# ScalarE copies a finished projection before it rounds the next weight piece

## The chip, the cores and the metric

The kernel runs on one core of one Trainium2 chip. The metric is device time in microseconds (us), the median of the runs. Three runs of the kernel before took 1799.23, 1800.72 and 1801.95 us; the median is 1800.72 us.

## What is computed

Two transformer stacks run one after the other on a sequence of 256 tokens of width 1024, batch 1, in fp32. The first has two layers, each with a mixer (compressed, selected and windowed attention, stick-breaking attention and forgetting attention), cross attention to a memory of 256 tokens, and a gated MLP of width 2816 with a causal convolution over three tokens. The second has a retention layer with a context of 256 tokens, then a layer whose mixer is a gated short convolution; both are followed by a SwiGLU MLP of width 2816. The parts that matter here:

```python
# first stack, MLP
u = causal_conv3(h @ w_up, conv_w) + conv_b
gate, val = u[..., :D_FF], u[..., D_FF:]
return (jax.nn.silu(gate) * val) @ w_down
# second stack, mixer of the second layer
b_gate, c_gate, xv = jnp.split(h @ w_in, 3, axis=-1)
return (b_gate * short_conv(c_gate * xv, w_conv)) @ w_out
# second stack, both MLPs
return (jax.nn.silu(h @ w1) * (h @ w3)) @ w2
```

## The kernel before, in words

Activations lie in SBUF with features on partitions and the 256 tokens on the free axis. All weights come as a stream of 532 pieces of 128x1024 fp32 (512 KB), which SyncE loads into a ring of eight slots (`ring`). TensorE multiplies in fp32r, so each piece and each activation is cut into a rounded upper part and a remainder. ScalarE rounds a piece into `WH[s]` (`split`, L447) and VectorE subtracts to get `WL[s]` (`split`, L813). There are two buffers of each, s = 0 and 1. The product takes upper times upper, upper times lower and lower times upper.

The work is a fixed table of 28 stages (`STAGES`). A stage that makes projections (`make` on TensorE) turns a piece into 128 output features: 8 x 2 matmuls with `WH[s]`, then 8 with `WL[s]`, into PSUM bank `proj[s]`, and then it raises `mm_done`. A step of the loop is two pieces, s = 0 and s = 1. Before a piece TensorE waits for `wh_ready` and for `bank_free[s]`; before the last eight matmuls it waits for `consumed`, which VectorE raises with `WL[s]`. A stage that adds (`add`: out, mo, down, ro, f2, co) accumulates in four other banks and has no projection to copy out. Where a stage starts on freshly normed activations, its first step runs both pieces interleaved (`fresh=True`).

Each engine runs its own written order. `weights` on ScalarE (the function that the change touches) does for each piece: wait for `mm_done`, run `before` where there is one, round the next piece of that s (`split`), run `evac` where there is one. The `evac` that the stages give:

- q, kv, mq, rq: copy `proj[s]` out (L483) and free the bank. rg: the same with Silu (L746). rk: 512 columns (L751).
- rv (`values`, L757): wait for TensorE's four transposes of the piece before, then copy 512 columns.
- up (`up_upper`, L479): at s = 0, round the previous step's product into FH. The taps `up` (L701, L704) are its `before`.
- f13 (`swiglu`): at s = 0, Silu of `proj[0]` (L725); at s = 1, wait for VectorE's product (`bank_free[1]`), then round it into FH (L728).
- cx (`conv_in`, L786): at s = 0, wait for the product of the step before, then copy `proj[0]` out.
- cb (`conv_upper`, L797): wait for VectorE's product of this piece (`bank_free[s]`), then round it into FH. Its `before` is `conv_gate` (L792).

The stage mkv has its own loop, which the change does not touch.

VectorE's `weights` does for each piece: `before` (in cb: two taps L1230 and the product L1233; in f13 at s = 1 the product L1134), `split` (which waits for `wh_ready`), `evac` (in cb and f13 the remainder FL, L1237 or L895), and in some stages a reduction over an extra piece for the modulation vectors (`ada`, L821, L823). In the last step of a stage both engines round the first two pieces of the next stage.

Of the kernel before, what the change touches and what calls it, by code (L numbers as in the profile page):

```python
# [55 lines left out]
def next_piece(st, i, s):  # L56

    return i * st["per"] + (st["base"] + s * (st["per"] // 2))
# [138 lines left out]
def transformer(nc, xT_d, memT_d, ctxT_d, cond_d, stream_d, vecs_d, const_d, rope1_d, rope2_d, decay_d,  # L197
# [5 lines left out]
    with ctx:  # L203
# [180 lines left out]
        def loop(eng, steps, step, chain=None, per=0, peel=False):  # L384


            if peel:
                step(0, False)
            if steps > 1:
                with eng.Fori(1 if peel else 0, steps - 1) as i:  # L390
                    if chain:
                        chain.enter(i, per)
                    step(i, False)
                if chain:
                    chain.leave(steps - 1)
            step(steps - 1, True)
# [43 lines left out]
        def _(act):  # L440
# [4 lines left out]
            def split(r, s):  # L445
                act.wait_ge(loaded, r + 1)
                A(WH[:, s, :], ring[:, r % RING, :], ACT.Copy).then_inc(wh_ready, 1)  # L447

            def weights(k, evac=None, per=0, peel=False, before=None, tail=None, after=None):


                st = TABLE[k]

                def step(i, last):
                    for s in range(2):
                        if last and s == 1 and tail:
                            tail()
                        act.wait_ge(mm_done, i * 2 + (st["p0"] + s + 1))
                        if before:
                            before(i, s)  # L460
                        if not last:
                            split(next_piece(st, i, s), s)
                        elif k + 1 < len(TABLE):
                            split(TABLE[k + 1]["r0"] + s, s)
                        if evac:
                            evac(i, s)
                if after:
                    for i in range(st["steps"]):
                        step(i, i + 1 == st["steps"])
                        after(i)  # L470
                else:
                    loop(act, st["steps"], step, chain, per, peel)
                if evac:
                    n["q"] += st["steps"]
# [1405 lines left out]
```

## Time and profile before

| | us |
|---|---|
| median of three runs | 1800.72 |
| the profiled execution's own time | 1801.96 |
| its span | 1800.0 |
| TensorE matmul busy | 1701.6 (95%) |
| VectorE busy | 1107.1 (62%) |
| ScalarE busy | 827.6 (46%) |
| rounding on ScalarE, L447, 436 pieces | 461.0, mean 1057 ns |
| remainder on VectorE, L813, 436 pieces | 533.0, mean 1223 ns |

Span and own time differ by 1.96 us, which lies around the first and the last instruction. The mean granted TensorE clock is 0.976 of full speed. Busy time of an engine is a sum over all stages; which engine binds has to be read stage by stage. In the rows below a start is in us from the span's start, a duration is in us, and the last bracket is the idle time of the engine ahead of the row and who ended it. A row with x1 is one instruction. Instructions of one engine overlap a little: the next starts about 0.1 us before the recorded end of the one ahead.

### The profile page before, as it was taken

To read this page: it belongs to the slowest core of one execution; us is meant where nothing else is said; L and a number is where in the kernel's file an instruction comes from. 1 tells how busy PE (TensorE), PEld (TensorE's weight loads), DVE (VectorE), ACT (ScalarE), POOL (GpSimd) and SP (SyncE) were. 2 spreads that over 40 slices of the span, in tenths; PEclk is the share of its full clock that TensorE was granted. 3 is DMA by queue.
4 is the path that set the end of the run, shared out by engine and by line. 5 is a ranking of instruction groups with operands and counts; after the bars stand their busy time and mean duration, and the time that the engine had idled before them with its cause. 6 is when DMAs were issued, how large, how long until landed. Compare 5 with 4: busy or idle time off the path is not lost.

```text
span 1800.0 us, 37316 instructions
## 1 busy us (share of the span) xinstructions
PE 1701.6 (95%) x12659; PEld 1554.6 (86%) x12678; DVE 1107.1 (62%) x1644; ACT 827.6 (46%) x1392; POOL 38.8 (2%) x43
## 2 busy tenths in 40 slices
PE   8989989999898998999979999799899999999998
PEld 6976869999797676999959888589799988989998
DVE  3536468888773645888866632447755564665544
ACT  4545556653453555665344322113544444454443
POOL 0020000000002000000000000200000000000000
PEclk9988999999998999999999999999999999999999
DMA  9520225558783021556927842116555674445551
GB/s 321 176 72 1 85 68 167 183 187 274 219 268 106 1 94 47 176 186 200 372 107 237 300 152 93 58 47 231 201 182 180 222 256 140 163 134 182 186 182 64
DMA packets 81229, 293.41 MB, mean 163 GB/s; under 512 B 9360, under 2 KB 10768, under 8 KB 80400
## 3 DMA queue, kind: packets, MB, share of 16 engines
q1 hardware_dynamic: 78768, 283.29, 46.4%
q10 hardware_dynamic: 2400, 9.27, 1.8%
q8 instruction: 42, 0.69, 0.2%
q14 instruction: 19, 0.16, 0.0%
HBM read 291.48 MB, written 1.05 MB: 163 GB/s over the span
## 4 chain that ended last, share of the span: by engine, by line
PE 77%; DVE 10%; ACT 6%; issue 4%; DVEq 1%; POOL 1%; ACTq 0%; SPq 0%; DMA 0%; POOLq 0%
PE projs L1316 51%; PE accs L1316 20%; PE ob L1316 4%; ACT WH L447 3%; DVE WL L813 1%; DVE rstd L899 1%; DVE ring L823 1%; PE projs L1505 1%; DVE scr L905 1%; DVE cprod L821 1%; ACT scr L489 1%; DVE AL L914 1%; ACT AH L507 0%; DVE x L837 0%; DMA ring<-in_stream 0%
## 5 line engine op out<-in xcount | busy, mean ns | idle before, releaser
L813 DVE TENSOR_TENSOR WL<-ring,WH 128x1024 fp32r<-128x1024 f32 x436 | 533.0, 1223 | 472.4 <-ACT WH L447 471.8
L447 ACT ACTIVATE WH<-ring 128x1024 fp32r (+1 forms) x436 | 461.0, 1057 | 606.7 <-PE projs L1316 376.6
L1316 PE MATMUL projs<-AH,WH 128*128 128x256 f32 (+1 forms) x2432 | 626.4, 295 | 30.3 <-ACT AH L507 9.6
L1316 PE MATMUL projs<-AL,WH 128*128 128x256 f32 (+1 forms) x2432 | 629.8, 296 | 1.3
L1316 PEld LDWEIGHTS projs<-AH,WH 128*128 128x128 f32 x2432 | 463.2, 193 | 46.6 <-issue 26.3
L1316 PEld LDWEIGHTS projs<-AL,WH 128*128 128x128 f32 x2432 | 462.8, 193 | 22.4 <-DVE AL L912 7.1
L1316 PE MATMUL projs<-AH,WL 128*128 128x256 f32 (+1 forms) x2432 | 361.9, 292 | 1.4 <-DVE WL L813 1.4
L1316 PEld LDWEIGHTS projs<-AH,WL 128*128 128x128 f32 x2432 | 325.9, 193 | 9.0 <-DVE WL L813 1.6
L1316 PE MATMUL accs<-FH,WH 128*128 (+1 forms) x768 | 187.8, 282 | 0.2
L1316 PE MATMUL accs<-FL,WH 128*128 (+1 forms) x768 | 187.9, 281 | 0.0
L1316 PEld LDWEIGHTS accs<-FH,WH 128*128 128x128 f32 x768 | 144.4, 188 | 1.1 <-issue 1.1
L1316 PEld LDWEIGHTS accs<-FL,WH 128*128 128x128 f32 x768 | 145.1, 189 | 0.0
L823 DVE SCALAR_TENSOR_TENSOR ring<-ring,crow 128x1024 f32 (+1 forms) x96 | 117.1, 1220 | 2.6
L1316 PE MATMUL accs<-FH,WL 128*128 (+1 forms) x768 | 112.2, 281 | 0.0
L1316 PEld LDWEIGHTS accs<-FH,WL 128*128 128x128 f32 x768 | 100.1, 189 | 0.0
L701 ACT ACTIVATE cv<-projs,vecs 128x256 f32<-128x256 f32 x88 | 49.6, 564 | 91.8 <-PE projs L1316 91.8
L1316 PE MATMUL ob<-scr,const 128*128 128x256 f32 x224 | 61.7, 428 | 18.4 <-ACT scr L489 17.6
L1316 PE MATMUL accs<-AH,WH 128*128 (+1 forms) x288 | 72.9, 286 | 2.5 <-DVE AL L970 1.9
L1316 PEld LDWEIGHTS ob<-scr,const 128*128 128x128 f32 x224 | 45.9, 214 | 31.2 <-ACT scr L489 24.2
L1316 PE MATMUL accs<-AL,WH 128*128 (+1 forms) x288 | 72.1, 283 | 0.0
L1316 PEld LDWEIGHTS accs<-AH,WH 128*128 128x128 f32 x288 | 55.2, 192 | 4.6 <-DVE AL L970 3.1
L1316 PEld LDWEIGHTS accs<-AL,WH 128*128 128x128 f32 x288 | 55.2, 192 | 0.0
(217 smaller groups left out, 1555.9 us busy)
## 6 DMA issues: line engine op xcount, KB each, us to landing
ring<-in_stream SPq DMA_DIRECT2D x532, 512.0 KB, 4.2
W1v<-in_w ACTq DMA_DIRECT2D x4, 512.0 KB, 8.1
W1k<-in_w ACTq DMA_DIRECT2D x4, 512.0 KB, 12.7
D<-in_decay ACTq DMA_DIRECT2D x4, 512.0 KB, 3.3
x<-in_xT SPq DMA_DIRECT2D x2, 512.0 KB, 5.2
memT<-in_memT SPq DMA_DIRECT2D x1, 1024.0 KB, 11.2
ctxT<-in_ctxT ACTq DMA_DIRECT2D x1, 1024.0 KB, 5.9
out_y<-ybuf SPq DMA_DIRECT2D x8, 128.0 KB, 2.0
```

The costliest lines, as they stand in the source:

```text
L447: A(WH[:, s, :], ring[:, r % RING, :], ACT.Copy).then_inc(wh_ready, 1)
L489: A(scr1[:, kb % 4, :], src[:, kb, :], ACT.Square).then_inc(sq_ready, 1)
L701: A(cv[:, s, :], proj[s][:, 0:S], ACT.Identity, bias=cb, scale=w2).then_inc(tap_ready, 1)
L813: V.tensor_tensor(WL[:, s, :], ring[:, r % RING, :], WH[:, s, :].bitcast(F32), ALU.subtract).then_inc(consumed, 1)
L821: chain.link(V.scalar_tensor_tensor(out=cprod[:], in0=piece, scalar=1.0, in1=crow_ctx[:], op0=ALU.mult, op1=ALU.mult, accum_out=modc[:, ba ...
L823: V.scalar_tensor_tensor(out=piece, in0=piece, scalar=1.0, in1=crow[:], op0=ALU.mult, op1=ALU.mult, accum_out=mod[:, bass.ds(j, 1)]).then_ ...
L899: chain.link(V.reciprocal((dst or rstd)[:], rms[:]))
L905: V.scalar_tensor_tensor(out=scr2[:, kb % 4, :], in0=src[:, kb, :], scalar=gain[:, kb:kb + 1], in1=by[:], op0=ALU.mult, op1=ALU.mult).then ...
L914: V.scalar_tensor_tensor(out=AL[:, kb, sel, :], in0=scr2[:, kb % 4, :], scalar=shift[:, kb:kb + 1], in1=hi, op0=ALU.add, op1=ALU.subtract) ...
L1316: return T.matmul(out, lhsT, rhs, start=start, stop=stop, skip_group_check=True)
L1505: ins = T.transpose(projs[:, g, dst:dst + 128], prob[:, g, src:src + 128], ident)
```

## The change

In `weights` on ScalarE the call of `evac` is moved ahead of the rounding of the next piece. The waits inside `evac` move with it, so that the rounding now stands behind them. Nothing else is changed; the order on TensorE, VectorE, GpSimd and SyncE is as it was.

```diff
                         act.wait_ge(mm_done, i * 2 + (st["p0"] + s + 1))
                         if before:
                             before(i, s)
+                        if evac:
+                            evac(i, s)
                         if not last:
                             split(next_piece(st, i, s), s)
                         elif k + 1 < len(TABLE):
                             split(TABLE[k + 1]["r0"] + s, s)
-                        if evac:
-                            evac(i, s)
```

## Rows read from the trace of the kernel before

**Rows 1.** The page: shares of the chain of waits by engine.

```profile
PE 77%; DVE 10%; ACT 6%; issue 4%; DVEq 1%; POOL 1%; ACTq 0%; SPq 0%; DMA 0%; POOLq 0%
```

**Rows 2.** Windows: busy us (instructions) per engine, granted clock, DMA share, GB/s.

```profile
1289.00:1411.00 122.00, 121.33 (x1011) 121.17 (x1010) 68.44 (x85) 57.31 (x86) 0.00 (x0) 1.00 0.56 180
...
1540.00:1563.00 23.00, 20.59 (x164) 19.66 (x163) 18.07 (x32) 12.21 (x20) 0.00 (x0) 1.00 0.41 140
```

**Rows 3.** Timeline of ScalarE in stage cb: start, duration, instruction, idle before.

```profile
1556.94 0.42 ACT L797 ACTIVATE FH<-prod 128x256 f32 x1 [1.84 <-DVE prod L1233]
1557.26 0.49 ACT L792 ACTIVATE cv<-CU,vecs 128x256 f32 x1
1557.66 1.04 ACT L447 ACTIVATE WH<-ring 128x1024 fp32r x1
```

**Rows 4.** Timeline of VectorE in stage cb.

```profile
1556.38 0.42 DVE L1233 TENSOR_TENSOR prod<-cv,projs 128x256 f32<-128x256 f32 x1
1556.72 1.22 DVE L813 TENSOR_TENSOR WL<-ring,WH 128x1024 fp32r<-128x1024 f32 x1
...
1558.70 0.48 DVE L1230 SCALAR_TENSOR_TENSOR cv<-CU,vecs,cv 128x256 f32<-128x256 f32 x1 [0.43 <-DVE FL L1237]
...
1559.89 0.42 DVE L1233 TENSOR_TENSOR prod<-cv,projs 128x256 f32<-128x256 f32 x1
...
1566.08 0.42 DVE L1233 TENSOR_TENSOR prod<-cv,projs 128x256 f32<-128x256 f32 x1
```

**Rows 5.** Timeline of TensorE at the start of stage co.

```profile
1565.30 1.11 PE L1316 MATMUL accs<-FH,WL 128*128 128x256 f32 x8
```

**Rows 6.** Timeline of all engines in stage f13, at s = 1.

```profile
1405.50 0.42 DVE L1134 TENSOR_TENSOR prod<-cv,projs 128x256 f32<-128x256 f32 x1 [0.36 <-PE projs L1316]
1405.54 1.06 ACT L447 ACTIVATE WH<-ring 128x1024 fp32r x1 [1.55 <-PE projs L1316]
...
1406.79 1.22 DVE L813 TENSOR_TENSOR WL<-ring,WH 128x1024 fp32r<-128x1024 f32 x1 [0.87 <-ACT WH L447]
...
1407.05 1.12 PE L1316 MATMUL projs<-AH,WL 128*128 128x256 f32 x8
```

**Rows 7.** Timeline at the first step of stage f13.

```profile
1289.41 0.36 ACT L725 ACTIVATE cv<-projs 128x256 f32<-128x256 f32 x1
1289.67 1.05 ACT L447 ACTIVATE WH<-ring 128x1024 fp32r x1
...
1289.83 0.39 PE L1316 MATMUL projs<-AH,WH 128*128 128x256 f32 x1 [0.67 <-ACT cv L725]
...
1290.87 0.41 DVE L1134 TENSOR_TENSOR prod<-cv,projs 128x256 f32<-128x256 f32 x1
```

**Rows 8.** Timeline of ScalarE and VectorE in stage up, at s = 0.

```profile
304.81 1.05 ACT L447 ACTIVATE WH<-ring 128x1024 fp32r x1
...
306.09 1.22 DVE L813 TENSOR_TENSOR WL<-ring,WH 128x1024 fp32r<-128x1024 f32 x1
...
307.94 0.48 DVE L1079 SCALAR_TENSOR_TENSOR cv<-projs,vecs,cv 128x255 f32<-128x255 f32 x1 [0.30 <-ACT cv L701]
```

**Rows 9.** Timeline of TensorE where it waits behind q, kv and rv.

```profile
499.74 1.21 PE L1316 MATMUL projs<-AH,WL 128*128 128x256 f32 x8 [1.35 <-DVE WL L813]
...
541.74 0.58 PE L1316 MATMUL projs<-AH,WH 128*128 128x256 f32 x1 [3.35 <-DVE AL L912]
...
1150.48 0.63 PE L1685 MATMUL accs<-const,scr 128*128 128x128 f32 x4 [2.22 <-DVE V L1155]
```

**Rows 10.** Timeline of ScalarE at the end of stage rv.

```profile
1148.38 0.58 ACT L757 ACTIVATE scr<-projs 128x512 f32<-128x512 f32 x1
```

**Rows 11.** Waits of TensorE over the span: total us, times, longest.

```profile
PE projs L1316 <- ACT P L483: 4.9, 2, 3.9
...
PE accs L1316 <- ACT mq L483: 0.9, 2, 0.5
```

**Rows 12.** Window at the start of stage mkv: columns as in Rows 2.

```profile
542.00:546.00 4.00, 4.00 (x20) 4.00 (x21) 0.00 (x0) 0.00 (x0) 0.42 (x1) 0.50 0.72 265
```

## Prediction

> **What bounds the kernel now.** I read the chain of waits first: 77% of it is TensorE [rows 1]. So a change on ScalarE costs or saves time only where TensorE runs out of work, and the question for each stage is how much time lies between a late piece and the matmul that needs it. The windows by stage say where that is. In f13, as in up, TensorE is busy 121.33 of 122.00 us with 1011 matmuls, 0.12 us each, so a piece of 24 matmuls takes 2.88 us and a step 5.76 us [rows 2]. In cb it is busy only 20.59 of 23.00 us [rows 2]: there it waits on something else. The timelines of single steps then give the order on ScalarE and VectorE.
>
> What a late WH[s] must meet: TensorE works on the other bank for 2.88 us after it has raised mm_done for s. Then it needs the new WH[s] and the freed bank, and 16 x 0.12 = 1.92 us later WL[s].
>
> **What the change removes, adds and moves.** No instruction is added or removed. The copy comes earlier by one rounding (about 0.96 us from start to start), the rounding later by the copy and by whatever wait stands in front of it. A 256-column ACTIVATE puts the next one 0.32 us later (1556.94 to 1557.26) [rows 3], a Silu of 256 columns 0.26 us [rows 7].
>
> *Plain copies (q, kv, rq, rg, mq; rk with 512 columns).* WH comes 0.26 us later (rk about 0.5), WL too. Against a cover of 2.88 us less one rounding that is nothing. In the first step of a stage, where TensorE waits for the copy (0.67 us idle at 1289.83) [rows 7], it needs WH as well: copy plus rounding have the same sum in either order. Cost 0. The exceptions are stage ends where TensorE is idle behind VectorE's last WL. Behind q of the second layer it waits 1.35 us for WL, and that WL ends a row of VectorE work that began with a WL after a rounding: +0.27 us. Behind both kv stages it waits for the last remainder AL, which VectorE makes after the last WL (3.35 us idle in the second layer, as much in the first): 2 x 0.28 us [rows 9]. Together +0.8 us.
>
> *mq, twice.* TensorE waits for the second copy, 0.9 us in both stages together [rows 11], and this wait goes. But VectorE's second WL comes 0.3 us later, and the first row maxima of the attention are queued behind it on VectorE. What is late next is these maxima: between -0.46 us and +0.3 us each; I take 0, since the two nearly meet.
>
> *up, 2 x 22 steps.* At s = 0 the FH rounding now stands ahead of the piece. The product is ready (the taps ahead of it have waited for it already). WH starts 0.31 us later, at 305.12, and ends 306.17; WL moves from 306.09 to about 306.35 [rows 8]. VectorE then idles 0.30 us before the next taps (307.94), and this hides the 0.26 us. TensorE needs WH only at 307.04. Cost 0. If the cover is gone, taps and product move by what is left over, still ahead of TensorE.
>
> *f13, 2 x 22 steps.* At s = 1 the piece now waits for the product, 1405.50 + 0.42. FH starts 0.14 us after it (as 1556.38 + 0.42 to 1556.94 in cb [rows 3, 4]), 1406.06; WH 1406.38 to 1407.44, instead of 1405.54 to 1406.60, 0.84 us later [rows 6]. TensorE's piece at s = 0 ends at 1407.05 + 1.12 = 1408.17, so 0.7 us are left in steady state (some 0.45 with the hop of a semaphore and the earlier issue of the weight load). WL moves from 1406.79 to 1407.63 and has 1.9 us more. Cost 0 per step. The first step is another case: the product at s = 1 stands behind WL of s = 0, which is 0.26 us late: 1291.13 to 1291.54, FH 1291.68, WH 1292.00 to 1293.05, at TensorE 1293.15. It is ready at 1289.83 + 2.88 = 1292.71 [rows 7]. +0.44 us, twice: +0.9 us.
>
> *cx.* The copy at s = 0 waits for the product of the step before, which is there as soon as the piece is. The chain of this stage runs over the rounding at s = 1, which has no evac. Its first step hands on about +0.15 us.
>
> *End of rv.* The copy waits for four transposes (0.63 us [rows 9]), then takes 0.58 us [rows 10], and the last WH and WL come behind it; TensorE waits 2.22 us for a V copy that stands behind this WL on VectorE [rows 9]. +0.9 us. Within rv a piece takes more than 5 us, and nothing is late.
>
> *cb, 8 pieces: the step that decides.* Here ScalarE now waits for VectorE's product before it rounds, and VectorE waits for the rounding before it makes WL. Two queues that ran side by side become one chain. Before: product 1556.38, WL 1556.72, FL, next taps 1558.70, next product 1559.89, 3.51 us from product to product, and WL started 0.34 us after the product since WH was long there [rows 4]. After: product ends +0.42, FH starts +0.56, WH +0.88, ends +1.92 [rows 3], and WL starts about 0.19 us after that, as in f13 (1406.60 to 1406.79 [rows 6]): +2.11. So WL, and behind it on VectorE FL, the next taps and the next product, come 1.77 us later per piece. FH, done earlier now, gives nothing back, since FL stood behind WL before, too. Seven such pieces lie ahead of the eighth product: it moves from 1566.08 [rows 4] to 1566.08 + 7 x 1.77 = 1578.5. The second piece of co is rounded 0.88 us after it starts and at TensorE 2.0 us after it: 1580.5. Before, TensorE began this piece at 1565.30 + 1.11 = 1566.41 [rows 5]. +14.1 us, and co is bound by TensorE from there, so nothing gives it back. Bounds of the unshown hops: 0.03 to 0.2 us from WH to WL, 0.26 to 0.42 us from FH to WH, that is 1.55 to 1.9 us per piece, +12.5 to +15 us.
>
> *Sum.* 0.8 + 0 + 0.9 + 0.15 + 0.9 + 14.1 = +16.8 us. Against the profiled execution's own time, 1801.96, that gives 1818.8; it lay 1.2 us above the median, so against the median 1817.5 us (+0.93%).
>
> **The clock.** After the idle 3.35 us at 541.74 the granted clock is 0.50, the 1.2 GHz level, and 20 matmuls take 4.00 us [rows 9, 12] where they take 2.4 us at full clock: 1.6 us lost in that window. In cb after the change TensorE would work 2.88 of 5.28 us and idle 2.4 us at a time, shorter than that, so I forecast full clock. Within cb a fall would mostly hide; at the start of co it would cost 1.6 to 3 us.
>
> **The rivals.**
> 1. *The clock falls in cb and stays low into co.* For it: half of each piece time becomes idle. Against it: each idle stretch is shorter than the 3.35 us of [rows 9]. 16.8 + 1.6 to 3, some 1820 us.
> 2. *cb is covered (not slower).* A piece is rounded one ahead, and a late WL in cb hides as it does in f13. Then only the edges count: 0.8 + 0.9 + 0.15 + 0.9 = +2.8 us less 0.9 us at mq, 1802.6 us. It holds as long as VectorE, not in wait for WH, has 1.77 us idle per piece. Against it: it idles 0.43 us before the taps, and this behind its own FL [rows 4].
> 3. *The bank is what counts.* TensorE's waits for copies (4.9 us for P, 0.9 us for mq [rows 11]) go with the earlier release, and cb is covered: about 1795 us. Against it: at P the same matmul needs WH, so the order there changes nothing. The Trainium skill, PSUM — Partial Sum Buffer, Summary: rules for kernel authors, says under its general entry to evacuate promptly, for want of room in the banks. By that the change is an improvement; only the mq rows of this trace bear it out.
> 4. *f13 loses in every step.* If hops were 0.5 us longer than the rows show, TensorE would wait at s = 1 of 42 steps; 0.1 us each is 4.2 us, so 1822 us or more.
>
> **How the numbers follow.** My forecast has 0.75 (own range 1814 to 1820), rival 1 0.10, rival 4 0.03, rival 2 0.07, rival 3 0.05. A change of 0.2% (3.6 us) is about the least that can be told from none here. Slower 0.88, same 0.07 (rival 2), faster 0.05. The time is that of my forecast, 1817.5 us. The range takes in the bounds of cb, the hops and rival 1: 1811 to 1823.
>
> **What the trace after would show.** In cb: ScalarE in the order gate, FH, WH; WL about 2.1 us behind the start of the product instead of 0.34; products 5.3 us apart; VectorE idle before WL, released by WH L447; TensorE idle some 2.4 us per piece; and the first matmuls of co 12 us later against their stage's start. In up and f13 the windows of 122 us unchanged, but for 0.4 us idle in f13's first step. rv's last V copy 0.9 us later. I am wrong if products in cb stay 3.5 us apart, if TensorE idles in the steady steps of up or f13, or if cx lengthens.

## The result, and the profile after

The changed kernel takes 1815.49 us (median of four runs, 1814.24 to 1816.07); the kernel before takes 1800.57 us, the median of the three runs named at the start and a fourth. The ratio is 1.0082, with a 95% interval of 1.0064 to 1.0099: slower by 14.9 us. Forecast were 1817.5 us and a range of 1811 to 1823.

| | before | after |
|---|---|---|
| median, us | 1800.57 | 1815.49 |
| profiled execution, own time | 1801.96 | 1815.33 |
| its span | 1800.0 | 1812.7 |
| TensorE busy | 1701.6 | 1705.5 |
| ScalarE busy | 827.6 | 828.2 |
| VectorE busy | 1107.1 | 1108.3 |

The engines do the same work; TensorE's 3.9 us more of busy time include some at a lower clock, told below. The chain of waits of the kernel after, by engine, has less of TensorE than [rows 1], and more of VectorE and ScalarE:

```profile
PE 75%; DVE 11%; ACT 7%; issue 4%; DVEq 1%; POOL 1%; ACTq 1%; SPq 0%; POOLq 0%
```

Stage cb on ScalarE after, against [rows 3]. The order is now FH, WH, gate. FH waited for the product before, too (1.84 us, now 3.53 us). What is new is that the rounding WH stands directly behind it:

```profile
1556.94 0.42 ACT L797 ACTIVATE FH<-prod 128x256 f32 x1 [3.53 <-DVE prod L1233]
1557.26 1.04 ACT L447 ACTIVATE WH<-ring 128x1024 fp32r x1
...
1559.04 0.51 ACT L792 ACTIVATE cv<-CU,vecs 128x256 f32 x1 [0.74 <-PE projs L1316]
```

The same piece on VectorE, against [rows 4]:

```profile
1556.39 0.42 DVE L1233 TENSOR_TENSOR prod<-cv,projs 128x256 f32<-128x256 f32 x1
1558.51 1.23 DVE L813 TENSOR_TENSOR WL<-ring,WH 128x1024 fp32r<-128x1024 f32 x1 [1.70 <-ACT WH L447]
1559.65 0.42 DVE L1237 TENSOR_TENSOR FL<-prod,FH 128x256 f32 x1
1560.81 0.48 DVE L1230 SCALAR_TENSOR_TENSOR cv<-CU,vecs,cv 128x256 f32<-128x256 f32 x1 [0.73 <-DVE FL L1237]
...
1561.99 0.42 DVE L1233 TENSOR_TENSOR prod<-cv,projs 128x256 f32<-128x256 f32 x1
...
1576.79 0.42 DVE L1233 TENSOR_TENSOR prod<-cv,projs 128x256 f32<-128x256 f32 x1
```

WL now starts 2.12 us after the start of the product (0.34 before) and has 1.70 us idle ahead of it, ended by WH. The rounding follows FH with no idle time, so its weight piece had already landed. The eight products lie 5.30, 5.61, 5.30, 5.60, 5.30, 5.00 and 4.50 us apart, where they were 3.50, 3.83, 3.50, 3.81, 3.51, 3.22 and 2.97 us apart. Before, what TensorE waited for in cb was the bank that VectorE's product frees:

```profile
1549.54 0.38 PE L1316 MATMUL projs<-AH,WH 128*128 128x256 f32 x1 [0.63 <-DVE prod L1233]
```

After, in cb and at the start of co, against [rows 5]:

```profile
1547.44 0.39 PE L1316 MATMUL projs<-AH,WH 128*128 128x256 f32 x1 [2.08 <-ACT WH L447]
1553.32 0.58 PE L1316 MATMUL projs<-AH,WH 128*128 128x256 f32 x1 [2.75 <-ACT WH L447]
...
1578.65 0.39 PE L1316 MATMUL accs<-FH,WH 128*128 128x256 f32 x1 [1.33 <-ACT WH L447]
```

It waits for the rounding ahead of five of the eight pieces of cb and of the first two of co. It doesn't wait ahead of the first two of cb, nor of the sixth: the fifth, at the lower clock, takes 5.29 us (1553.32 to 1558.61) and fills the gap.

The times between two landmarks of a profile are a finer measure than the runs. VectorE makes each reciprocal of a norm once, so the time between two of them is the time of a stretch. The stretch cx, cb, co lies between the reciprocal at 1480.87 and the one at 1591.66. The chain of waits of the kernel before has them as below (a row of the chain begins where the one ahead ends, so it can be 0.1 us shorter than the instruction):

```profile
1480.87 1.76 DVE rstd L899
1591.66 1.67 DVE rstd L899
```

and that of the kernel after as

```profile
1479.27 1.76 DVE rstd L899
1604.17 1.67 DVE rstd L899
```

that is 110.79 and 124.90 us: +14.11 us. In a second profile of the changed kernel it is 124.91. The other stretches, in us, with the kernels of the experiments below:

| stretch (stages in it) | before | after | only_cb | all_but_cb |
|---|---|---|---|---|
| q to out, layer 0 | 211.37 | 209.47 | 210.35 | 210.85 |
| mq, mo, layer 0 | 37.64 | 37.53 | 37.72 | 37.57 |
| up, down, layer 0 | 206.40 | 206.43 | 206.47 | 206.55 |
| q to out, layer 1 | 203.15 | 203.23 | 203.16 | 203.31 |
| mq, mo, layer 1 | 37.61 | 37.49 | 37.65 | 37.53 |
| up, down, layer 1 | 204.58 | 204.61 | 204.57 | 204.60 |
| rq to ro | 343.40 | 343.62 | 343.42 | 343.56 |
| f13, f2, first | 202.85 | 203.02 | 202.84 | 203.03 |
| cx, cb, co | 110.79 | 124.90 | 124.91 | 110.83 |
| f13, f2, second | 200.28 | 200.47 | 200.29 | 200.45 |

The first row differs by up to 1.9 us between these kernels and follows no edit. In only_cb every other stretch without an edit is within 0.1 us of before.

### The profile page after: what moved, and what is told of

Its sections match the earlier page's. It is cut to its first block, busy times and chain, and to the rows that moved or that the text cites. A ratio compares the mean times of both kernels' runs of the same rounds, so it can differ in the third digit from the quotient of the medians.

```text
span 1812.7 us, 37266 instructions
## 1 busy us (share of the span) xinstructions
PE 1705.5 (94%) x12659; PEld 1557.7 (86%) x12678; DVE 1108.3 (61%) x1644; ACT 828.2 (46%) x1392; POOL 39.4 (2%) x43
## 4 chain that ended last, share of the span: by engine, by line
PE 75%; DVE 11%; ACT 7%; issue 4%; DVEq 1%; POOL 1%; ACTq 1%; SPq 0%; POOLq 0%
PE projs L1316 49%; PE accs L1316 20%; PE ob L1316 4%; ACT WH L447 4%; DVE WL L813 2%; DVE rstd L899 1%; DVE scr L905 1%; PE projs L1505 1%; ACT scr L489 1%; DVE cprod L821 1%; DVE ring L823 1%; DVE AL L914 1%; ACT AH L507 1%; SPq L419 0%; DVE cv L1230 0%
## 5 line engine op out<-in xcount | busy, mean ns | idle before, releaser
L728 ACT ACTIVATE FH<-prod 128x256 f32 (+1 forms) x44 | 18.4, 418 | 99.7 <-DVE prod L1134 99.7
```

The source lines that it names most:

```text
L728: A(FH[:, step, :], prod[:], ACT.Copy).then_inc(fh_ready, 1)
```

## The experiments

The reasons to be told apart: (a) the price lies in cb alone, where rounding, which had run beside VectorE's product, now waits for it; (b) it is spread over all stages; (c) it is the copy's own duration; (d) it is the clock. Open as well is why f13, where rounding waits for a product too, costs next to nothing.

**only_cb: the changed order in cb alone.** In this and the next kernel `weights` has an argument `first`.

```diff
-            weights(K + 8, conv_upper, before=conv_gate)
+            weights(K + 8, conv_upper, before=conv_gate, first=True)
```

> The order is changed in stage cb alone; all other stages keep the order of the kernel before. Theory (the chain in cb is the whole price): products in cb 5.3 us apart instead of 3.5, the second piece of co starts 13.8 us later, time +13 to +14.5 us against before. Rival (the price is spread over all stages that make projections, cb a part of it): less than +8 us.

Measured: 1814.78 against 1800.26 us, +14.5 us, ratio 1.0077 (1.0063 to 1.0091), at the upper end of what was expected. The stretch with cb takes 124.91 us, products are 5.3 and 5.6 us apart as in the changed kernel, and no other stretch moves by more than 0.1 us but the first.

**all_but_cb: the changed order everywhere else.**

> The order is changed in every stage that the change touches except cb. Theory: only the edges count, +0.3 us at the start of each f13, +1.0 at the end of rv, +0.27 behind each kv, -0.26 at the end of rg: +1 to +3 us. Rival (spread over all stages): +7 us or more.

Measured: 1801.10 us, +0.8 us, ratio 1.0004 (0.9994 to 1.0013). No difference that the runs can tell, and a little under the expected 1 to 3 us; the stretches behind the first add up to 0.7 us more than before. The stretch with cb is back at 110.83 us. So (b) falls, and the two halves of the edit (14.5 and 0.8 us) add up to the whole (14.9 us) within the spread of the runs.

**wait_alone: the wait ahead of the rounding, the copy behind it.**

```diff
 def conv_gate(i, s):
     A(cv[:, s, :], CU[...], ...).then_inc(tap_ready, 1)
+    act.wait_ge(bank_free[s], i + (q2 + 2))
 def conv_upper(i, s):
-    act.wait_ge(bank_free[s], i + (q2 + 2))
     A(FH[:, i * 2 + s, :], prod[:], ACT.Copy).then_inc(fh_ready, 1)
```

> The kernel before, but in cb ScalarE waits for VectorE's product ahead of the rounding of the next piece and rounds FH behind it, as before. Theory (what costs is the wait for the product, which joins two queues into one chain): WL starts 1.79 us after the product instead of 0.34, +1.45 us per piece, +11.6 us in all. Rival (what costs is the copy, 0.32 us put ahead of each of eight roundings): the wait alone costs under 3 us.

Measured: 1813.49 us, +13.2 us, ratio 1.0072 (1.0059 to 1.0086); the stretch grew by 12.36 us, products 5.11 and 5.42 us apart. Its ScalarE in cb:

```profile
1557.20 1.06 ACT L447 ACTIVATE WH<-ring 128x1024 fp32r x1 [3.34 <-DVE prod L1233]
1558.17 0.40 ACT L797 ACTIVATE FH<-prod 128x256 f32 x1
1558.47 0.50 ACT L792 ACTIVATE cv<-CU,vecs 128x256 f32 x1
```

12.36 of 14.11 us come with the wait alone; the copy ahead of the rounding adds 1.75 us. So (c) falls as the main cause. 12.36 is a little over the expected 11.6. Part of that is that the rounding starts 0.24 us after the product's end here (1557.20 against 1556.54 + 0.42), where FH had started 0.14 us after it: 0.8 us in eight pieces.

**fl_first: on VectorE FL ahead of WL, on the changed kernel.**

```diff
-            weights(K + 8, conv_lower, per=4, before=conv_gate)
+            def conv_both(i, s):
+                conv_gate(i, s)
+                conv_lower(i, s)
+            weights(K + 8, lambda i, s: None, per=4, before=conv_both)
```

> The changed kernel, and in cb VectorE makes the remainder FL directly behind the product, ahead of WL. FH is there 1.0 us after the product starts, so FL runs while ScalarE still rounds the piece, and WL is all that stands behind the rounding. Theory (in cb the chain product, FH, WH, WL, FL, taps is serial, and FL can leave it): products 4.5 us apart instead of 5.3, +9 to +10 us against before instead of +14.9. Rival (the wait of ScalarE alone sets the pace, what VectorE does behind it is hidden): +14 to +15 us.

Measured: 1808.48 us against 1800.15 us, +8.3 us, ratio 1.0043 (1.0029 to 1.0057), somewhat under the expected 9 to 10 us; the stretch takes 118.97 us (+8.18). Its VectorE in cb:

```profile
1552.22 0.42 DVE L1233 TENSOR_TENSOR prod<-cv,projs 128x256 f32<-128x256 f32 x1
1553.34 0.42 DVE L1237 TENSOR_TENSOR FL<-prod,FH 128x256 f32 x1 [0.71 <-ACT FH L797]
1554.34 1.23 DVE L813 TENSOR_TENSOR WL<-ring,WH 128x1024 fp32r<-128x1024 f32 x1 [0.57 <-ACT WH L447]
1555.48 0.48 DVE L1230 SCALAR_TENSOR_TENSOR cv<-CU,vecs,cv 128x256 f32<-128x256 f32 x1
```

Products are 4.45 us apart. WL still starts 2.12 us behind the product, as in the changed kernel. What has gone is the part behind it: from WL to the next product it is 2.32 us instead of 3.17 or 3.48, since FL and VectorE's idle time behind FL (0.43 or 0.73 us) now fall into the wait for the rounding. So the rounding is on the chain, and what VectorE had queued behind it was, too. This is the chain shown from its other end.

**after_again and cb_fill.** The changed kernel on one chip with three others, and the changed kernel with six matmuls on zeros behind each piece of cb:

```diff
                         ins.then_inc(mm_done, 1)
+                        turn_over(fill)
...
-            make(K + 8, X(AH), X(AL))
+            make(K + 8, X(AH), X(AL), fill=6)
```

> The changed kernel once more, on the same chip as the next three: +14 to +16 us against before.

> The changed kernel, and TensorE runs six 512-column matmuls on zeros after each piece of cb (1.3 us in an idle stretch of 2.1 us). The granted clock of 1550 to 1560 us should be 1.00 instead of 0.66. Theory (the fallen clock in cb is hidden, since TensorE waits for the rounding anyway): same time as the changed kernel within 0.5 us. Rival (the clock is part of the price): 1.5 to 3 us faster than the changed kernel.

Measured: 1816.03 and 1816.29 us against 1801.10 us before, +14.9 and +15.2; stretch with cb 124.91 and 124.88 us. The window 1550 to 1560 us of the changed kernel and of cb_fill (columns as in [rows 2], the granted clock third from the end):

```profile
1550.00:1560.00 10.00, 7.25 (x38) 7.04 (x38) 5.74 (x10) 3.63 (x6) 0.00 (x0) 0.66 0.31 103
```

```profile
1550.00:1560.00 10.00, 8.30 (x58) 6.28 (x56) 5.47 (x10) 2.86 (x5) 0.00 (x0) 1.00 0.32 105
```

The clock does fall to its lower level in cb after the change, and giving it back changes nothing: (d) falls. The slow piece has this effect: it ends after the next rounding is there, and ScalarE's gate waits 0.74 us for it (1559.04 above). But the gate is done at 1559.55, and VectorE's taps, which need it, wait for FL until 1560.81 anyway.

**f13_one_more and f13_three_more: how much cover f13 has.** The order is changed in both f13 stages only, and at s = 1 one or three more copies stand in front of FH.

```diff
+                        for _ in range(1):        # 3 in the other kernel
+                            A(scr1[:, _ + 1, :], prod[:], ACT.Copy)
                         A(FH[:, step, :], prod[:], ACT.Copy).then_inc(fh_ready, 1)
```

> The kernel before with the changed order in both f13 stages only, and at s = 1 one more copy of the product into an unused tile ahead of FH (0.32 us). Theory (the cover in f13 is about 0.55 us): steady steps stay 5.76 us, only the first step pays, +1.0 to +1.5 us in all. Rival (the cover is used up already): 42 steps x 0.3 us, +12 us.

> As the one before, but three more copies (0.97 us). Theory: the cover of 0.55 us is exceeded, WH comes 3.2 us after the end of the last piece of its bank, a step takes 6.3 us instead of 5.76, +22 to +26 us in all. Rival (f13 has more room than the 0.55 us): under +10 us.

Measured: one more, 1801.33 us, +0.2 us, ratio 1.0002 (0.9993 to 1.0012), less than the expected 1.0 to 1.5 us, which the runs could hardly tell from none; three more, 1820.34 us, +19.2 us, ratio 1.0104 (1.0088 to 1.0119). The first f13 stretch takes 203.23 us with one (+0.38) and 211.96 us with three (+9.11), the second 200.66 and 209.50 us. Steady steps with one more copy, all engines:

```profile
1349.11 0.42 DVE L1138 TENSOR_TENSOR prod<-cv,projs 128x256 f32<-128x256 f32 x1 [0.30 <-PE projs L1320]
...
1350.19 1.04 ACT L447 ACTIVATE WH<-ring 128x1024 fp32r x1
...
1350.65 1.12 PE L1320 MATMUL projs<-AH,WL 128*128 128x256 f32 x8
1351.43 1.23 DVE L817 TENSOR_TENSOR WL<-ring,WH 128x1024 fp32r<-128x1024 f32 x1 [1.90 <-ACT WH L447]
```

WH ends at 1351.23, and TensorE's run on the other bank at 1351.77: still ahead. With three:

```profile
1345.92 0.42 DVE L1138 TENSOR_TENSOR prod<-cv,projs 128x256 f32<-128x256 f32 x1 [0.52 <-PE projs L1320]
...
1347.47 1.12 PE L1320 MATMUL projs<-AH,WL 128*128 128x256 f32 x8
1347.62 1.04 ACT L447 ACTIVATE WH<-ring 128x1024 fp32r x1
...
1348.72 0.19 PEld L1320 LDWEIGHTS projs<-AH,WH 128*128 128x128 f32 x1 [0.33 <-ACT WH L447]
...
1352.07 0.42 DVE L1138 TENSOR_TENSOR prod<-cv,projs 128x256 f32<-128x256 f32 x1 [0.51 <-PE projs L1320]
```

WH ends at 1348.66, behind the end of the other piece at 1348.59. So TensorE waits for it in every step, and a step takes 6.15 us instead of 5.76. So f13 has the same join of two queues as cb at s = 1, and its steady steps pay nothing as long as it stays under its cover. The cover comes out as 3 x 0.31 - 0.39 = 0.54 us. The expected 22 to 26 us were too many: they took a step of 6.3 us, +0.54. With the cover of 0.55 us that the same expectation names, three copies give 3 x 0.31 - 0.55 = +0.38 us, which is what a step grew by; the 6.3 us did not follow from it.

**cx_product_first and cx_and_cb: another order on VectorE.** Both start from the kernel before; the second has both edits.

```diff
-            weights(K + 7, conv_in)
+            weights(K + 7, lambda i, s: None, before=conv_in)
...
+                dve.wait_ge(fl2_ready, i * 2 + (n["gated"] + s))
                 V.tensor_tensor(prod[:], cv[:, s, :], proj[s][:, 0:S], ALU.mult).then_inc(bank_free[s], 1)
...
                 V.tensor_tensor(FL[:, i * 2 + s, :], prod[:], ...).then_inc(fl2_ready, 1)
-                dve.wait_ge(fl2_ready, i * 2 + (n["gated"] + s + 1))
```

> The kernel before, and in cx VectorE makes the product CU ahead of WL at s = 1 instead of behind it. The 0.34 us that TensorE waits for CU in each step goes, a step takes 5.76 us instead of 6.32: -3 to -4 us. Rival (the rounding on ScalarE is what is late): within 0.5 us of before.

> As the one before, and in cb VectorE waits for its own FL not behind it but ahead of the next product, after the next taps. The idle 0.43 or 0.73 us per piece goes, products 3.0 to 3.1 us apart instead of 3.5 and 3.8: another -3 to -4 us, -6 to -8 us in all against before, faster than both kernels.

Measured: 1797.85 us, -2.3 us, ratio 0.9985 (0.9976 to 0.9994); and 1795.49 us, -4.7 us, ratio 0.9973 (0.9962 to 0.9984). The stretch takes 107.41 us (-3.38) and 105.05 us (-5.74); a step of cx 5.76 us, the products in cb 3.06 to 3.14 us apart from the second to the sixth. The stretch of the first is as expected; the second gains 2.4 us more, not 3 to 4, and stays short of the expected 6 to 8 us in all. Both are faster than the kernel before by more than the interval, if by little. The runs show some 1 us less than the stretches, which is within their interval. With both edits TensorE is busy nearly from end to end, as the window of cx_and_cb shows:

```profile
1500.00:1550.00 50.00, 49.72 (x409) 49.05 (x409) 30.76 (x42) 23.36 (x34) 0.00 (x0) 1.00 0.54 178
```

So cb and cx had been bound by the order on VectorE: the stage that paid for the change was one where VectorE, which the change made wait, already set the pace.

## Why the prediction was right, point by point

- *The place and the mechanism: right.* Two queues that ran side by side became one chain, in cb alone. only_cb and all_but_cb show the place, wait_alone the wait, fl_first the chain. WL was forecast 2.11 us behind the product's start and came 2.12 us behind it; +1.77 us per piece was forecast, and the pieces of the loop show +1.78 to +1.80. Against the reciprocal ahead of them, the eighth product comes 12.31 us later (7 x 1.77 = 12.4 forecast), the second piece of co 14.00 us later (14.1 forecast), and the stretch is 14.11 us longer. The agreement to a tenth is in part luck. The last interval grew by 1.53 us and not 1.77, and the forecast took TensorE's start on that piece before at 1566.41, the recorded end of the row ahead; its first matmul starts at 1566.25.
- *up: right.* 206.40 and 206.43 us; layer 1, 204.58 and 204.61. VectorE's idle time hid the later WL, as said: the 0.30 us ahead of the taps [rows 8] are used up in the kernel after (FL 305.51 to 305.93, taps at 305.94).
- *f13, steady: right.* In the kernel after, WH at s = 1 ends at 1353.98 and TensorE's other piece at 1354.73, 0.75 us left where 0.7 was forecast:

```profile
1352.94 1.04 ACT L447 ACTIVATE WH<-ring 128x1024 fp32r x1
1353.61 1.12 PE L1316 MATMUL projs<-AH,WL 128*128 128x256 f32 x8
```

  The part of it that can be used is the 0.54 us of f13_three_more, against 0.45 forecast with the hops.
- *f13, first step: mis-sized.* Forecast +0.44 us each; the stretches grew by 0.17 and 0.19. Part of it is a gain that I had put at zero. "Copy plus rounding have the same sum in either order", but TensorE waits less where the rounding comes last. On TensorE before it was idle 0.67 us there [rows 7], after 0.54 us. The second piece then starts 3.20 us behind the first, 0.32 us later than its 2.88 us, and not 0.44:

```profile
1287.91 0.38 PE L1316 MATMUL projs<-AH,WH 128*128 128x256 f32 x1 [0.54 <-ACT WH L447]
1291.11 0.39 PE L1316 MATMUL projs<-AH,WH 128*128 128x256 f32 x1
```

  0.32 less 0.13 is the 0.19 us of the stretch.
- *cx: mis-sized, by little.* Forecast +0.15 us; the first product of cb comes 0.04 us later against the reciprocal ahead of it.
- *End of rv and of kv: right in place and size, but given back nearby.* TensorE's waits after, against 1.35, 3.35 and 2.22 us in [rows 9]:

```profile
497.70 1.21 PE L1316 MATMUL projs<-AH,WL 128*128 128x256 f32 x8 [1.52 <-DVE WL L813]
...
539.97 0.57 PE L1316 MATMUL projs<-AH,WH 128*128 128x256 f32 x1 [3.62 <-DVE AL L912]
...
1149.22 0.63 PE L1685 MATMUL accs<-const,scr 128*128 128x128 f32 x4 [3.21 <-DVE V L1155]
```

  They are +0.17, +0.27 and +0.99 us (forecast 0.27, 0.28 and 0.9). Yet the stretch rq to ro grew by 0.22 us only, and q to out of layer 1 by 0.08. At the end of rg the wait of 0.26 us for the Silu is gone, which I had not put in the sum, so TensorE was 0.72 us late behind the V copy. The trace shows where most of that came back: in the rotation of Q that follows, where TensorE waits for VectorE. The first matmul of K's rotation is level again, 224.88 us behind the reciprocal at 934.62 before and 224.89 us behind the one at 932.63 after:

```profile
1159.50 1.13 PE L1316 MATMUL accs<-K,rope 128*128 128x256 f32 x4 [0.57 <-DVE Q L1182]
1157.52 1.13 PE L1316 MATMUL accs<-K,rope 128*128 128x256 f32 x4 [0.80 <-DVE Q L1182]
```

  (the first row is of before, the second of after). Where it came back behind q and kv of the second layer no experiment shows; that stays open.
- *mq: near.* Taken at 0, the stretches are 0.11 and 0.12 us shorter.
- *The sum.* Without cb I had +2.7 us; the stretches behind the first one give +0.49 (14.60 less 14.11), the runs of all_but_cb +0.8. This is the term of the sum that was mis-sized: it took each late row at a stage end as late for good. It makes up the difference of 1.9 us between +16.8 forecast and +14.9 measured, as far as the runs can tell; the interval of all_but_cb goes from -1.1 to +2.3 us.
- *The clock: wrong in what it would do, right in what it costs.* I forecast full clock in cb, since each idle stretch would be shorter than 3.35 us; it was 0.66 over 10 us, and cb_fill shows that it cost nothing. Rival 1 would have had co start late by it. It did not: the stretch is 124.90 us with the fall and 124.88 without.
- *Rivals 2 and 3 are out* by the result and by only_cb, *rival 4* by the f13 stretches (+0.17 and +0.19 us) and by f13_one_more. Where the Trainium skill, PSUM — Partial Sum Buffer, Summary: rules for kernel authors, asks to evacuate promptly, the runs show no gain in the whole from it here: all_but_cb, with the earlier copies of all other stages, has no difference that the runs can tell (only the two short stretches with mq are 0.1 us shorter), and in cb the bank itself was freed by VectorE, so that moving ScalarE's work could not free it sooner.

## What to carry to other kernels

Before two pieces of work on an in-order engine are swapped, look at the wait inside each one. A copy whose input is ready delays the work behind it by its own 0.3 us or so, which was mostly hidden here. A copy that waits for another engine ties the work behind it to that engine, and if that engine in turn waits for this work, two parallel queues become a chain. Price it stage by stage. The cover is the time that is left between the delayed piece and the moment its user needs it. Here the same join cost nothing per step in a stage with 0.5 us of cover to spare, and 14 us in eight pieces of a stage with none.

## What the runs showed of the hardware

- In cb after the change TensorE was idle for 1.08, 2.08 and 2.75 us, with about 3 us of work between. Then the granted clock fell to its 1.2 GHz level, though no idle stretch was as long as the 3.35 us of [rows 9], by which I had held it safe. The matmul at 1553.32 took 0.58 us instead of 0.39. With matmuls on zeros in the idle time (cb_fill) the clock of the same window is 1.00. The window in the kernel after:

```profile
1553.00:1559.00 6.00, 5.68 (x26) 5.68 (x27) 3.44 (x6) 1.77 (x4) 0.00 (x0) 0.50 0.26 87
```

- The first stretch, q to out of layer 0, in which the clock changes level several times, took between 208.87 and 211.88 us over twelve profiles, with no relation to the edits. It goes with the granted clock. Where this was 0.90 in the window 20 to 145 us, the stretch took 208.87 to 209.47 us, at 0.89 it took 210.31 to 210.86, and at 0.88 it took 211.37 and 211.70; one profile (fl_first, 0.90, 211.88 us) does not fit. That the clock is the cause was not tested. All other stretches without an edit in them repeat within 0.2 us, save rq to ro, which was 0.8 us shorter in two of them. The medians of the unchanged kernel beside the experiments were 1800.15, 1800.26 and 1801.10 us, so a microsecond between two medians need not come from a change.
